# V projected in its own pair, and parts of the output projection in the last pair of an attention stage

## What is computed

```python
k = (rmsnorm(h, kv_norm_g) @ w_k)                 # shared K and V, 16 heads of 64
v = (rmsnorm(h, kv_norm_g) @ w_v)
q = (rmsnorm(h, norm_mix_g[1]) @ b_w_q[0])
z = q k^T * HEAD_DIM ** -0.5 + bias               # per head
log_rest = where(causal, log_sigmoid(-z), 0)
after = cumsum(log_rest, reverse=True) - log_rest
a = where(causal, exp(log_sigmoid(z) + after), 0)
h = h + (a @ v) @ b_w_o[0]                        # then the second SwiGLU and the final norm
```

## Time and profile before

| | before |
|---|---|
| median of 3 runs | 2781.6 us (2779.8 to 2782.3) |
| the profiled execution | 2782.98 us |
| its span, first to last instruction | 2781.3 us |
| mean granted TensorE clock | 0.978 |
| TensorE busy | 2681.6 us, 96% of the span |
| VectorE, ScalarE, GpSimd busy | 48%, 27%, 36% |
| DMA traffic | 220.18 MB, 79 GB/s on average |

### The profile page before, as it was taken

The page is one execution under the profiler, slowest core; times in us unless marked ns, Lnnn a source line. Parts: engine busy times, 40 slices in busy tenths (PEclk is TensorE's granted clock), DMA queues, the critical chain, the costliest instruction groups (busy, mean ns, idle before and its releaser), DMA issues.

```text
span 2781.3 us, 42516 instructions
## 1 busy us (share of the span) xinstructions
PE 2681.6 (96%) x16785; PEld 2564.6 (92%) x16785; DVE 1327.5 (48%) x1343; ACT 763.3 (27%) x1096; POOL 1008.4 (36%) x534
## 2 busy tenths in 40 slices
PE   7999999999999999999999999969999999999997
PEld 6989999999999999988888888749999999999997
DVE  5244453333333333678878878782533333333335
ACT  5112110000000000367767767661200000000003
POOL 4643475667676777000000000020433333333330
PEclk8999999999999999999999999879999999999998
DMA  3111133333333333423222222222211111111111
GB/s 116 46 39 32 45 91 95 115 114 115 114 115 114 114 114 118 165 66 100 82 74 79 83 86 83 93 101 86 61 46 46 47 46 47 46 47 46 40 38 63
DMA packets 247794, 220.18 MB, mean 79 GB/s; under 512 B 12842, under 2 KB 211298, under 8 KB 247586
## 3 DMA queue, kind: packets, MB, share of 16 engines
q1 hardware_dynamic: 229090, 206.75, 23.8%
...
## 4 chain that ended last, share of the span: by engine, by line
PE 90%; DVE 5%; ACT 2%; issue 2%; ACTq 0%; DMA 0%; SPq 0%; DVEq 0%
PE ps L762 50%; PE ps L891 18%; PE aux L1021 8%; PE ps L973 3%; PE ps L946 2%; PE ps L928 2%; PE ps L958 2%; PE aux L992 1%; DVE scratch L1686 1%; PE aux L1027 1%; DVE v_all L1714 1%; PE aux L981 1%; PE aux L1061 0%; PE ps L842 0%; DVE sp_part_odd L1841 0%
## 5 line engine op out<-in xcount | busy, mean ns | idle before, releaser
L644 POOL TENSOR_TENSOR w_hi<-w_raw,ones_col 128x1024 fp32r<-128x1024 f32 x140 | 270.9, 1935 | 821.5 <-PE ps L762 536.6
L651 POOL TENSOR_TENSOR w_lo<-w_raw,w_hi 128x1024 fp32r<-128x1024 f32 x156 | 436.0, 2795 | 12.2
L762 PE MATMUL ps<-near_hi,w_hi 128*128 128x352 f32 x1632 | 357.7, 327 | 15.7 <-DVE near_lo L1673 12.1
L762 PE MATMUL ps<-near_lo,w_hi 128*128 128x352 f32 x1632 | 354.5, 325 | 0.0
L762 PE MATMUL ps<-near_hi,w_lo 128*128 128x352 f32 x1632 | 352.5, 324 | 0.0
L762 PEld LDWEIGHTS ps<-near_hi,w_hi 128*128 128x128 f32 x1632 | 279.3, 190 | 20.0 <-issue 12.0
L762 PE MATMUL ps<-in_hi,w_hi 128*128 128x352 f32 x1320 | 286.9, 325 | 3.7 <-issue 3.7
L1800 DVE TENSOR_TENSOR h<-h,ps 128x1056 f32<-128x1056 f32 x160 | 200.1, 1251 | 188.0 <-PE ps L891 187.8
L762 PE MATMUL ps<-in_lo,w_hi 128*128 128x352 f32 x1320 | 285.5, 324 | 0.0
L762 PE MATMUL ps<-in_hi,w_lo 128*128 128x352 f32 x1320 | 284.3, 323 | 0.0
L718 POOL TENSOR_TENSOR in_lo<-o_back,in_hi 128x1056 fp32r<-128x1056 f32 x7 | 18.1, 2589 | 732.6 <-ACT in_hi L1254 732.6
...
## 6 DMA issues: line engine op xcount, KB each, us to landing
w_raw<-in_w_gate_dram SPq DMA_DIRECT2D x44, 512.0 KB, 4.4
w_raw<-in_w_up_dram SPq DMA_DIRECT2D x44, 512.0 KB, 4.0
w_raw<-in_w_down_dram SPq DMA_DIRECT2D x44, 512.0 KB, 3.8
...
w_hi<-kept_hi SPq DMA_DIRECT2D x32, 512.0 KB, 3.7
w_lo<-kept_lo SPq DMA_DIRECT2D x32, 512.0 KB, 4.6
w_raw<-in_a_w_in_dram SPq DMA_DIRECT2D x16, 512.0 KB, 3.9
```

Source lines behind the costliest of these rows:

```text
L644: gp.tensor_tensor(hi, raw, one, ALU.mult).then_inc(w_hi_done, 1)
L651: gp.tensor_tensor(lo, raw, as32(hi), ALU.subtract).then_inc(w_ready, 1)
L762: last = mm(out[:, c, 0:CH], w[:, ks], x[:, k, c * CH:c * CH + CH], start=(k == 0 and n == 0), stop=(k == KT - 1 and n == 2))
```

## The change

V of a pair is projected in the pair itself and no longer in the one before. Ahead of pair 0 only K and Q are projected. In `pair(p)` the chunks c0 to c2 are V of p, c3 to c5 K and c6 to c8 Q of p + 1. V's chunks are taken in the order 2, 1, 0, and V's split is in three parts. The order of the calls on TensorE, ScalarE and VectorE is written anew.

The last pair has an order of its own, `last_pair`, which holds what the call with `now=False` held too. After V's chunks and turns it has nine units u0 to u8: output tiles 2, 1 and 0, three column chunks of 352 each, over the first six of the eight k (pairs 0 to 5). Each is 18 matmuls in the shared bank, and VectorE adds it into h (`unit_added`). VectorE now makes the low parts of the returned results (`o_low`), and GpSimd makes none. h tiles 2, 1, 0 are loaded back earlier. The output projection then takes tiles in the order 3, 0, 1, 2, 4, ..., 7; tiles 0, 1, 2 have only k = 6 and 7 left. SP's order of loads follows. K's first rows lie in `sp` instead of `staged`, so the first two `capped` wait for their store.

```diff
+V_CHUNKS = (2, 1, 0)
+V_PARTS = ((6, 8), (3, 6), (0, 3))
-X_ORDER = [("c", 0), ("p", 0), ("c", 1), ("k", 0), ("p", 1), ("k", 1), ("c", 2), ("p", 2), ("c", 3), ("k", 2),
-           ("c", 4), ("p", 3), ("c", 5), ("c", 6), ("c", 7), ("v", 0), ("c", 8), ("v", 1), ("v", 2)]
+X_ORDER = [("c", 0), ("p", 0), ("v", 2), ("c", 1), ("p", 1), ("v", 1), ("c", 2), ("v", 0), ("p", 2), ("c", 3),
+           ("k", 0), ("c", 4), ("p", 3), ("k", 1), ("c", 5), ("k", 2), ("c", 6), ("c", 7), ("c", 8)]
+
+X_LAST = [("c", 0), ("p", 0), ("v", 2), ("c", 1), ("p", 1), ("v", 1), ("c", 2), ("v", 0), ("p", 2), ("u", 0),
+          ("u", 1), ("p", 3), ("u", 2), ("u", 3), ("u", 4), ("u", 5), ("u", 6), ("u", 7), ("u", 8)]
+U_TILES = (2, 1, 0)
+U_K = 6
+O_ORDER = (3, 0, 1, 2, 4, 5, 6, 7)
...
@@ SP, last pair @@
+            sync.wait_ge(h_kept, 16 * KT)
+            sync.wait_ge(in_ready, 32 + 6)
+            sync.dma_start(h[:, 2, :], h_dram[2]).then_inc(h_back[2], 16)
+            sync.dma_start(h[:, 1, :], h_dram[1]).then_inc(h_back[1], 16)
+            slab(R_O + U_TILES[2], R_O + U_TILES[2], 0, unit_done, NC)
+            sync.wait_ge(in_ready, 32 + 7)
+            sync.dma_start(h[:, 0, :], h_dram[0]).then_inc(h_back[0], 16)
             sync.wait_ge(z_done, NS * PAIRS)
             sync.wait_ge(s_scored, 4 * PAIRS)
-            for n in range(KT):
+            for n in range(3, KT):
                 sync.dma_start(h[:, n, :], h_dram[n]).then_inc(h_back[n], 16)
+            slab(R_O + 3, R_O + 3, 1, unit_done, 2 * NC)
...
@@ GpSimd @@
-            for n in range(PAIRS - 1):
-                o_low(n)
...
@@ TensorE @@
+                elif kind == "u":
+                    n, chunk = U_TILES[r // NC], r % NC
+                    pe.wait_ge(slab_in[n % 2], 32 * (R_O // 2 + (2 if n == 0 else 1)))
+                    pe.wait_ge(in_ready, 32 + U_K)
+                    hi, lo = slab_slot(R_O + n)
+                    for k in range(U_K):
+                        ks = slice(k * P, k * P + P)
+                        for m, (w, x) in enumerate(((hi, in_hi), (hi, in_lo), (lo, in_hi))):
+                            last = mm(xb[:, 0:CH], w[:, ks], x[:, k, chunk * CH:chunk * CH + CH],
+                                      start=(k == 0 and m == 0), stop=(k == U_K - 1 and m == 2), skip_group_check=True)
+                    last.then_inc(unit_done, 1)
...
-            for n in range(3):
-                pe.wait_ge(slab_in[n % 2], 32 * (n // 2 + 1))
+            for n in range(2):
+                pe.wait_ge(slab_in[n], 32)
...
+            pe.wait_ge(unit_out, NC * len(U_TILES))
+
+            for i, n in enumerate(O_ORDER):
...
+                first_k = U_K if n in U_TILES else 0
+                for k in range(first_k, KT):
...
@@ VectorE @@
+            def o_low(n):
+                low(32 + n, o_back[:, n % 3, :], n)
+
+            def unit_added(a):
+                n, chunk = U_TILES[a // NC], a % NC
+                cols = slice(chunk * CH, chunk * CH + CH)
+                dve.wait_ge(h_back[n], 16)
+                dve.wait_ge(unit_done, a + 1)
+                vec.tensor_tensor(h[:, n, cols], h[:, n, cols], aux[:, 0, 0:CH], ALU.add).then_inc(unit_out, 1)
```

More of the change, by code:

```diff
@@ new lines, in pair @@
+                carry(p, c, 4)
+                scores(p, c, 7)
+                take_later(p, c, 5)
+                sample_scores(p, c, 3)
+                values(p, c, 4)
+                carry(p, c, 5)
+                x_turn(p, c, ("c", 5), True)
+                scores(p, c, 8)
+                take_later(p, c, 6)
+                values(p, c, 5)
+                x_turn(p, c, ("k", 2), True)
+                scores(p, c, 9)
+                carry(p, c, 6)
+                x_turn(p, c, ("c", 6), True)
@@ L1968, in pair @@
+                softplus(p, c, 1)
+                logits(p, c, 0)
+                softplus_high(p, c, 1)
+                capped(p, c, 2)
+                softplus_low(p, c, 1)
                 if past:
                     out(q, 0)
-                if now:
-                    softplus(p, c, 2)
-                    softplus_high(p, c, 2)
-                    softplus_low(p, c, 2)
-                    capped(p, c, 3)
-                    a_low(p, c, 1)
-                if more:
-                    chunk_evicted(p, c, 2)
@@ L1999, in pair @@
-                if more:
-                    chunk_evicted(p, c, 4)
-                if now:
-                    logits(p, c, 4)
-                    softplus(p, c, 5)
-                    softplus_high(p, c, 5)
-                    softplus_low(p, c, 5)
-                if more:
-                    k_low(p, c, 2)
-                if now:
-                    a_low(p, c, 4)
-                    capped(p, c, 6)
-                if more:
-                    k_low(p, c, 3)
-                    chunk_evicted(p, c, 5)
@@ L2034, in pair @@
-                if more:
-                    chunk_evicted(p, c, 7)
-                if now:
-                    logits(p, c, 7)
-                    softplus(p, c, 8)
-                if more:
-                    k_low(p, c, 5)
-                if now:
-                    sample_softplus(p)
-                    softplus_high(p, c, 8)
-                    softplus_low(p, c, 8)
-                    a_low(p, c, 7)
-                    capped(p, c, 9)
-                if more:
-                    chunk_evicted(p, c, 8)
@@ L2049, in pair @@
[L2049 to L2063 removed]
+                logits(p, c, 1)
@@ new lines, in pair @@
+                a_low(p, c, 0)
+                v_low(p, 0)
+                softplus(p, c, 2)
+                capped(p, c, 3)
+                chunk_evicted(p, c, 2, True)
+                softplus_high(p, c, 2)
+                softplus_low(p, c, 2)
+                v_low(p, 1)
+                a_low(p, c, 1)
+                logits(p, c, 2)
+                softplus(p, c, 3)
+                softplus_high(p, c, 3)
+                capped(p, c, 4)
+                softplus_low(p, c, 3)
+                a_low(p, c, 2)
@@ new lines, in pair @@
+                chunk_evicted(p, c, 3, True)
+                softplus(p, c, 4)
+                v_low(p, 2)
+                logits(p, c, 3)
+                softplus_high(p, c, 4)
+                capped(p, c, 5)
+                softplus_low(p, c, 4)
+                a_low(p, c, 3)
+                chunk_evicted(p, c, 4, True)
+                softplus(p, c, 5)
+                logits(p, c, 4)
+                softplus_high(p, c, 5)
+                capped(p, c, 6)
+                softplus_low(p, c, 5)
@@ new lines, in pair @@
+                a_low(p, c, 4)
+                logits(p, c, 5)
+                softplus(p, c, 6)
+                sample_capped(p)
+                softplus_high(p, c, 6)
+                capped(p, c, 7)
+                softplus_low(p, c, 6)
+                a_low(p, c, 5)
+                chunk_evicted(p, c, 5, True)
+                logits(p, c, 6)
+                softplus(p, c, 7)
+                k_low(p, c, 0)
+                capped(p, c, 8)
+                softplus_high(p, c, 7)
+                a_low(p, c, 6)
@@ new lines, in pair @@
+                softplus_low(p, c, 7)
+                k_low(p, c, 1)
+                capped(p, c, 9)
+                chunk_evicted(p, c, 6, True)
+                logits(p, c, 7)
+                k_low(p, c, 2)
+                softplus(p, c, 8)
+                softplus(p, c, 9)
+                softplus_high(p, c, 8)
+                softplus_high(p, c, 9)
+                softplus_low(p, c, 8)
+                a_low(p, c, 7)
+                softplus_low(p, c, 9)
+                logits(p, c, 8)
@@ new lines, in pair @@
+                sample_softplus(p)
+                capped(p, c, 10)
+                k_low(p, c, 3)
+                a_low(p, c, 8)
+                chunk_evicted(p, c, 7, True)
+                logits(p, c, 9)
+                softplus(p, c, 10)
+                softplus_high(p, c, 10)
+                capped(p, c, 11)
+                k_low(p, c, 4)
+                softplus_low(p, c, 10)
+                chunk_evicted(p, c, 8, True)
+                out(p, 1)
+                softplus(p, c, 11)
```

951 lines of the change are left out of this document (550 added, 401 removed).

## The result

| | before | after |
|---|---|---|
| median | 2780.7 us (4 runs, 2777.86 to 2782.3) | 2749.61 us (4 runs, 2747.39 to 2751.49) |
| ratio | | 0.9891, 95% interval 0.9877 to 0.9904 |
| the profiled execution | 2782.98 us | 2751.45 us |

The account below looks back on a forecast made before the run. TensorE's own work was taken as the bound, except in the last pair, bound by the chain scores, ScalarE, VectorE, TensorE. Gains 12.6 + 0 + 27.5 + 10.8 = 50.9 from 2781.6 gave 2730.7 us, range 2722 to 2750.

Parts of the forecast that it names:

- The sign: Whole kernel: faster than before, chance 0.95.
- Parts 1 and 3: Front, V projected in its own pair: gain 12.6 us; output loop, three tiles losing six of eight k: 27.5 us.
- The contention behind Part 4: Last stretch: with GpSimd's subtractions moved to VectorE, 11 us of slowed VectorE operations go; VectorE's sum is 86 us.
- Part 4, TensorE's work: Stretch from pair 6's end to the output loop: TensorE has 88.6 us of work and remains the bound.
- Part 4, waits: Last stretch: 0.8 us for unit 8's addition, 3.3 at values(2), 2 for small waits; stretch 95 us, gain 10.8.
- Part 4, the clock: Last stretch: TensorE's work priced at full clock, the profile to show a clock above 0.9.
- The rival of the low clock: Clock stays low in the last pair: 2770 us, or 2750 with half the stretch slow; chance 0.05.
- The first rival: Chain still sets the last stretch through VectorE's results: stretch 102 to 106 us, total 2737 to 2742; chance 0.17.
- The second: Rival: the new order costs the seven ordinary pairs 1 to 3 us each, total 2737 to 2752; chance 0.14.
- Part 2: New order of calls in pairs 0 to 6, V's path taken as covered: 0 us, range -7 to +14.
- an ordinary pair of 83.8 us (wrong if above 85): Pairs 0 to 6: the profile after would show an ordinary pair still taking 83.8 us.
- the forecast stretch: Last stretch, from pair 6's end to the output loop: 95 us, against 105.8 before.

Follow-up runs that it names:

- e6: Changed kernel with loads of rows 3 to 5 first, weights(1) and a_low(1) earlier, and the low part's seven subtractions back on GpSimd: 2749.59 us.
- e1: Changed kernel with SyncE issuing the loads of rows 3 to 5 ahead of the second four K pages and slab 1: 2742.79 us.
- e2: Changed kernel with only slab 1 (1 MB) moved behind the loads of rows 3 to 5, K pages still ahead: 2743.19 us.
- e4: Changed kernel with filler matmuls, results unused, on TensorE in the last pair: 22 ahead of values(1), 48 ahead of scores(5); 2744.68 us.
- e7: Changed kernel with the slab that follows chunk 8 issued behind the next pair's V pages in pairs 0 to 6: 2747.62 us.
- e13: Best order found (2736.40 us), with VectorE's subtractions of rows 1 to 5 cut from 1056 to 8 columns: 2737.36 us.
- e14: Best order found (2736.40 us), with ScalarE's casts of rows 1 to 5 cut from 1056 to 8 columns: 2735.93 us.
- e12: Best order found (2736.40 us), with 25 filler matmuls before scores(5) and the start of the sample scores moved behind it: 2737.02 us.

## Why the prediction was wrong

- **The sign, and Parts 1 and 3:** right, each within 0.5 us (12.6 and 27.5).
- **The contention behind Part 4:** right. 11 us claimed, 10.3 measured (e6). VectorE was given 86 and had 83.6.
- **Part 4, TensorE's work:** 88.6 claimed, 89.4 measured. +0.8.
- **Part 4, waits:** the step that failed. I allowed 0.8 + 3.3 + 2 = 6.1; the profile has 11.9, +5.8. The 3.3 was put at `values(2)` behind VectorE's queue. The real waits came from ScalarE: 2.8 us at `values(1)`, where `weights(1)` stood behind three casts and two DMA issues, and 6.2 at `scores(5)`, behind a load. I checked slab 3 and the h loads for cover and never walked SyncE's queue for `o_back` 3 to 5: eight K pages (8.12 us of issue) and a slab stand ahead of row 3. e1 removes that wait; e2 shows most of it to be the slab.
- **Part 4, the clock:** the second part of the failed step. It was taken as full. 97.2 - 89.4 = 7.8 us of busy time went to it, and e4 puts 6.5 us of the stretch on it. Together 0.8 + 5.8 + 7.8 = 14.4 against the 14.1 missing (94.7 was rounded to 95).
- **The rival of the low clock** had the mechanism, at a chance of 0.05, and its time for half of the stretch slow, 2750, is the time measured. That is luck: 23 us of the 109 were slow, not half, and the rest of the miss is waits and the ordinary pairs.
- **The first rival** (the chain and VectorE's queue hold the stretch at 102 to 106) was wrong in mechanism and size: VectorE was not the bound, and the stretch grew to 109. **The second** (1 to 3 us a pair) is met at its lower end, with 0.8 us a pair.
- **Part 2:** 0 claimed, inside -7 to +14 came +5.8. Two pieces are seen: 3.8 us of waits for p0's copy, where before had 0.7; and loop jumps each 1 us longer. e7 wins the latter back and some more. Against the statement "an ordinary pair of 83.8 us (wrong if above 85)" stand 84.1 to 84.5 us for pairs 2, 4 and 6, but 85.3 for pair 1.
- **The best order found** stays 3.5 us over the forecast stretch. It is not VectorE's nor ScalarE's work alone (e13, e14), and a filler doesn't win it (e12). Whether both relieved at once, or real work for TensorE in place of the filler, would reach 95 was not tried and stays open.
